# Streaming encoder step: the input projection cut into 36 units, with cache keys, gate recurrences and first queries between them

## The reference, cut to what matters

```python
# x: 64 sample rows + 16 meta rows + padding, then 1024 prompt rows (9 tiles of 128)
z = rms_norm(x, g_attn) @ w_in           # 1024 -> 1960 columns: cq, ckv, kr, gates, mq, mk, mv, mo
k, v = mla_keys_values([cache_ckv, rms_norm(z.ckv)], [cache_krope, rope(z.kr)])  # 1024 cached rows
q = rms_norm([q_nope, rope(q_rope)])     # from rms_norm(z.cq) @ w_uq
att = softmax(q k^T * scale, chunk-causal) v
b = cumsum(logf); m = running max(b, ig) # mLSTM gates, per 64-row chunk, 4 heads
h = mlstm_chunks(mq, mk, mv, ig, logf, state)
x = x + [att, rms_norm(h) * sigmoid(mo)] @ w_out
x = x + moe(rms_norm(x))                 # 32 experts, top 2
```

## Time and profile before

| | us |
|---|---|
| median of 3 runs | 1435.95 (1429.99 to 1442.3) |
| the profiled execution's own time | 1430.49 |
| its span, first to last instruction | 1428.7 |
| cache keys, to the projection's first matmul | 0 to 51.8 |
| projection | 51.8 to 294.8 |
| gates and first queries, to the first scores | 294.8 to 344.2 |
| attention and the rest | 344.2 to 1428.7 |

### The profile page before, as it was taken

One profiled execution on the slowest core, in us unless ns is written; L12 is line 12 of the kernel. 1 busy time (PEld: TensorE's weight loads), 2 busy tenths in 40 slices (PEclk: granted clock), 3 DMA queues, 4 the chain that ended last, 5 costly groups with the idle time before them and its releaser, 6 DMA issues.

```text
span 1428.7 us, 37955 instructions
## 1 busy us (share of the span) xinstructions
PE 1284.4 (90%) x16430; PEld 968.5 (68%) x16430; DVE 426.9 (30%) x873; ACT 333.7 (23%) x775; POOL 229.9 (16%) x318
## 2 busy tenths in 40 slices
PE   5899999955899999999999859999898989988995
PEld 2444444423666567666567559999898988988985
DVE  2210001036555446445444651111111111111110
ACT  4310010023544445454454200000001001000010
POOL 3100000003221222122120111111112111111101
PEclk9999999976989999999999979999999999999998
DMA  8012111050120122012030946999999999999992
GB/s 304 15 43 86 43 43 71 28 209 26 51 75 16 60 76 76 16 61 70 4 123 21 416 148 238 362 371 373 362 376 375 386 378 381 381 378 376 381 391 76
DMA packets 39709, 273.74 MB, mean 192 GB/s; under 512 B 9208, under 2 KB 13176, under 8 KB 27340
## 3 DMA queue, kind: packets, MB, share of 16 engines
q1 hardware_dynamic: 32944, 253.78, 45.9%
q0 software_dynamic: 6400, 17.84, 5.2%
q10 hardware_dynamic: 288, 1.05, 0.2%
HBM read 246.32 MB, written 30.48 MB: 194 GB/s over the span
## 4 chain that ended last, share of the span: by engine, by line
PE 69%; DMA 14%; issue 7%; DVE 4%; ACT 3%; POOL 2%; SPq 1%; POOLq 0%; ACTq 0%; DVEq 0%
PE psum L795 17%; PE psum L1058 16%; DMA arena<-in_w 12%; PE psum L1084 9%; PE psum L910 7%; PE psum L949 4%; PE psum L981 3%; PE psum L961 2%; PE psum L749 2%; PE psum L855 2%; PE psum L1094 1%; PE psum L764 1%; PE psum L1049 1%; POOL small L1461 1%; PE psum L896 1%
## 5 line engine op out<-in xcount | busy, mean ns | idle before, releaser
L1058 PE MATMUL psum<-arena 128*64 128x80 f32 (+1 forms) x8192 | 330.3, 243 | 31.3 <-DMA arena<-in_w 28.0
L1058 PEld LDWEIGHTS psum<-arena 128*64 128x64 f32 x8192 | 319.6, 142 | 41.6 <-issue 37.3
L795 PE MATMUL psum<-arena 128*128 128x512 f32 (+1 forms) x576 | 238.1, 574 | 0.6 <-DVE arena L1672 0.6
L795 PEld LDWEIGHTS psum<-arena 128*128 128x128 f32 x576 | 108.8, 190 | 124.2 <-issue 124.2
L1084 PE MATMUL psum<-arena 128*64 128x80 f32 (+1 forms) x4096 | 158.8, 239 | 5.3 <-issue 5.3
L1084 PEld LDWEIGHTS psum<-arena 128*64 128x64 f32 x4096 | 155.0, 139 | 6.1 <-issue 6.1
L910 PE MATMUL psum<-arena 128*128 128x512 f32 x288 | 127.0, 594 | 1.7 <-DVE arena L1912 1.0
L1418 ACT ACTIVATE arena<-psum,slot_gate 96x1024 f32<-96x1024 f32 x32 | 35.5, 1111 | 354.6 <-PE psum L1094 354.6
L749 PE MATMUL psum<-ident,arena 128*128 128x128 f32 (+1 forms) x432 | 65.2, 286 | 46.9 <-DVE arena L1766 18.2
L910 PEld LDWEIGHTS psum<-arena 128*128 128x128 f32 x288 | 53.3, 190 | 63.0 <-issue 61.4
L749 PEld LDWEIGHTS psum<-ident,arena 128*128 128x128 f32 (+1 forms) x432 | 50.8, 139 | 64.4 <-DVE arena L1653 19.8
(11 more groups left out here) (233 smaller groups left out, 1280.2 us busy)
## 6 DMA issues: line engine op xcount, KB each, us to landing
arena<-in_w SPq DMA_DIRECT2D x96, 2048.0 KB, 17.3
arena<-in_x_rows SPq DMA_DIRECT2D x18, 512.0 KB, 5.5
z_rows<-arena SPq DMA_DIRECT2D x9, 980.0 KB, 4.5
arena<-in_w_in SPq DMA_DIRECT2D x1, 7840.0 KB, 23.4
arena<-z_rows SPq DMA_DIRECT2D x9, 768.0 KB, 5.8
arena<-in_w_out SPq DMA_DIRECT2D x1, 4096.0 KB, 17.1
out_y<-arena SPq DMA_DIRECT2D x8, 512.0 KB, 2.6
xn_rows<-arena SPq DMA_DIRECT2D x8, 512.0 KB, 3.0
```

What stands on the lines that cost most here:

```text
L795: ins = pe.matmul(o[:, 0:hi - lo], xT[s][:, k, :], w_in[:, k, lo:hi], start=(k == 0), stop=(k == KD - 1))
L1058: ins = pe.matmul(o[c:c + CT, j * EB:j * EB + rows], w[:, k, j * P + c:j * P + c + CT], x[:, k, 0:rows], start=(k == 0), stop=(k == KD - 1))
```

## The change

The loop of the projection is replaced by 37 steps, i from -1 to 35. Step i has unit i (a tile of rows times one column chunk) and the small work `early(i)`. Units 0 to 8 are chunk 0 of the nine tiles, units 9 to 35 the other chunks, tile by tile. Steps -1 to 7 hold the cache keys, 1 to 9 the gate transposes of each tile, 11 to 18 the gate arithmetic, 19 to 28 the first tile's queries and keys and the decays (`cd`). Rows arrive transposed from DRAM (`xT_rows`) beside the plain rows, so `x_transposes` is gone; DVE scales them in SBUF (`xT_scale`). `w_in` comes chunk by chunk. Plain rows are still loaded for their squares, now by ACT's own DMA queue. Even units are emptied by ACT, odd ones by DVE, through four banks, and stored one by one. `w_out`, `g_mh` and `w_route` are loaded only after the last unit; the waits for them go to n = 1.

```diff
+UNITS = [(n, 0) for n in range(NT)] + [(n, c) for n in range(NT) for c in (1, 2, 3)]
+UBANK = (0, 1, 2, 4)
...
+def early(i):
+    if i < 0:
+        return cache_step(0) + cache_step(1)
+    m = NC
+    return (cache_step(i + 2) if i < NC else []) + [("ga", i - 1)] * (1 <= i <= NT) + {
+        19: [("cd", 0), ("cqT", 0), ("cn", 0)], 20: [("ckvT", m)], 21: [("q0", 0), ("q1", 0)],
+        22: [("kn", m), ("v", m), ("qsum", 0), ("ksum", m)], 25: [("kq", m)], 26: [("qTa", 0), ("qTb", 0)],
+        27: [("kTa", m), ("kTb", m), ("cqT", 1)], 28: [("cn", 1)],
+    }.get(i, [])
...
         @block.sync
+            load_xT(0)
+            load_w(0)
+            load_xT(1)
+            for dst, src in ((g_cq, "g_cq"), (g_ffn, "g_ffn"), (g_qk[:, 0:1], "g_q"), (g_qk[:, 1:2], "g_k"), (b_gate, "b_gate"),
+                             (mstate, "state_m")):
+                sp_.dma_start(dst, T[src]).then_inc(gains_in, 16)
+            sp_.dma_start(b_route, T["b_route"].to_broadcast([P, NG + NE])).then_inc(gains_in, 16)
+            sp_.dma_start(gate_rows, T["gate_rows"]).then_inc(gate_in, 16)
+            load_xT(2)
+            load_xT(3)
...
+            for n in range(4, 7):
+                load_xT(n)
+            load_w(1)
...
+            load_w(2)
+            load_w(3)
...
+            for i, (n, c) in enumerate(UNITS):
+                lo, hi = Z_CHUNKS[c]
+                wait_unit_read(sp_, i)
+                sp_.dma_start(z_dram[n * P:(n + 1) * P, lo:hi], zst[i % 4][:, 0:hi - lo]).then_inc(z_out[i % 4], 16)
+                if i == 17:
+                    sp_.wait_ge(z_full, 18)
+                    sp_.wait_ge(x_ssq, NT)
+                    sp_.wait_ge(kk_ok, NC)
+                    unit_stored(0)
+                    load_latents(0)
+                    sp_.dma_start(w_uq, T["w_uq"].rearrange("(k p) n -> p k n", p=P)).then_inc(wuq_in, 16)
...
+            sp_.wait_ge(z_full, len(UNITS))
+            sp_.dma_start(g_mh, T["g_mh"].to_broadcast([P, HM * DV])).then_inc(gmh_in, 16)
             sp_.dma_start(w_out, T["w_out"].rearrange("(k p) n -> p k n", p=P)).then_inc(wout_in, 16)
...
         @block.tensor
+            def z_unit(i):
+                n, c = UNITS[i]
+                w, at_ = chunk_width(c), KD * Z_CHUNKS[c][0]
+                pe.wait_ge(xT_ok, n + 1)
+                pe.wait_ge(win_in[c], 16)
+                if i >= 4:
+                    wait_unit_read(pe, i - 4)
+                o = unit_bank(i)
+                for k in range(KD):
+                    ins = pe.matmul(o[:, 0:w], xT[n][:, k, :], w_in[:, at_ + k * w:at_ + (k + 1) * w],
+                                    start=(k == 0), stop=(k == KD - 1))
+                ins.then_inc(z_full, 1)
...
+            for i in range(-1, len(UNITS)):
+                if i >= 0:
+                    z_unit(i)
+                for key in early(i):
+                    step(key)
...
         @block.scalar
+            load_x(0)
+            load_x(1)
+            for i in range(-1, len(UNITS)):
+                if i >= 0 and i % 2 == 0:
+                    z_take(i)
+                for key in early(i):
+                    fill_work(key)
+                if i < 0:
+                    x_squares(0)
+                if 1 <= i + 2 < NT:
+                    if i + 3 < NT:
+                        load_x(i + 3)
+                    x_squares(i + 2)
+                if i == 11:
+                    gate_logs()
+                if i == 18:
+                    gate_exps()
...
         @block.gpsimd
+            for i in range(-1, len(UNITS)):
+                if i < 0:
+                    kv_rstd_of(0)
+                    row_rstd(0)
+                if i + 2 <= NC:
+                    row_rstd(i + 2)
+                if 0 <= i and i + 1 < NC:
+                    kv_rstd_of(i + 1)
+                for key in early(i):
+                    pool_work(key)
...
         @block.vector
+            def xT_scale(n):
+                dve.wait_ge(xT_in[n], 16)
+                TT(xT[n], xT[n], bc(g_attn, [P, KD, P]), ALU.mult).then_inc(xT_ok, 1)
...
+            for i in range(-1, len(UNITS)):
+                if 0 <= i < NC:
+                    kv_norm(i)
+                if i >= 0 and i % 2:
+                    z_take(i)
+                if i < 0:
+                    for n in range(3):
+                        xT_scale(n)
+                elif i + 3 < NT:
+                    xT_scale(i + 3)
+                if i + 1 < NC:
+                    kv_sums(i + 1)
+                if i == 12:
+                    scale_gains()
+                if i == 13:
+                    gates_log()
+                if i == 14:
+                    gates_max()
+                if i == 16:
+                    gates_rows()
+                if i == 17:
+                    gates_end()
...
+                    if (n, h) == (1, 0):
+                        dve.wait_ge(wout_in, 32)
                         link(TT(w_route, w_route, bc(g_ffn, [P, KD, NG + NE]), ALU.mult))
```

More of the change, by code:

```diff
@@ L177, in pe_fills @@
     order = []
-    for c in range(NC + 2):
-        order += cache_step(c)
-    for n in range(-1, NT + 1):
+    for i in range(-1, len(UNITS)):
+        order += [key for key in early(i) if key[0] not in NO_BANK]
+    for n in range(NT + 1):
         if n >= 1:
@@ L193, in pe_fills @@
     return fills, used
+def early(i):
[7 more added lines that the diff above has]
+    }.get(i, [])
 def filler(n, h):
-    now, nxt, old = 0 <= n < NT, n + 1 < NT, n >= 1
+    now, nxt, old = n < NT, n + 1 < NT, n >= 1
     m = NC + n + 1
[L207 to L212, removed]
     return {
@@ L321, in build @@
         A = Area(7 * PART)
-        w_out = A(KD, D)
+        mlstm_at = A.at
+        qb, kb = A(HM, P), A(HM, P)
+        kw = kb
+        vaug = A(HM, CAUG)
+        chunk_mask = A(P)
+        state_at = A.at
+        state = [A(HM, CAUG) for _ in range(2)]
         w_route = A(KD, NG + NE)
-        after_weights = A.at
         mixT = A(KD, P)
@@ L343, in build @@
         g_mh = A(HM * DV)
[L344 to L349, removed]
+        w_out_at = ARENA - KD * D
+        assert A.at <= w_out_at, A.at
+        w_out = Area(w_out_at)(KD, D)
         A = Area(mixing)
@@ L531, in ahead, with unit_bank, chunk_width, wait_unit_read @@
             return value if isinstance(value, int) else eng.snap(value)
[L533 to L545, removed]
+        def unit_bank(i):
+            return bank(UBANK[i % 4])
+        def chunk_width(c):
+            return Z_CHUNKS[c][1] - Z_CHUNKS[c][0]
+        def wait_unit_read(eng, i):
+            eng.wait_ge(zd_read if i % 2 else za_read, i // 2 + 1)
         def load_part(eng, dst, src, row, signal):
@@ L607, in _ @@
[L607 to L618, removed]
@@ L845, in step @@
                     key_values(n, what)
+                elif what == "ga":
+                    wait_unit_read(pe, n)
+                    o = open_bank(key)
+                    for g in range(2):
+                        ins = pe.transpose(o[0:HM, g * P:(g + 1) * P], gat[:, n, g * HM:(g + 1) * HM], ident[:])
+                    filled(ins, key)
+                elif what == "cd":
+                    pe.wait_ge(g_ok, 1)
+                    pe.wait_ge(mixw_in, 16 * 4)
+                    o = open_bank(key)
+                    for h in range(HM):
+                        ins = pe.matmul(o[:, h * NCH:(h + 1) * NCH], pick[:, h, :], dec4, start=True, stop=True)
+                    filled(ins, key)
                 elif what == "cqT":
@@ new lines, in z_take @@
+            def z_take(i):
+                n, c = UNITS[i]
+                act.wait_ge(z_full, i + 1)
+                act.wait_ge(x_rstd, n + 1)
+                if i >= 4:
+                    act.wait_ge(z_out[i % 4], 16 * (i // 4))
+                o, w = unit_bank(i), chunk_width(c)
+                if c == 0:
+                    act.activation(gat[:, n], o[:, Z_GATE:Z_GATE + 2 * HM], ACT.Copy, scale=xrs[:, n:n + 1])
+                act.activation(zst[i % 4][:, 0:w], o[:, 0:w], ACT.Copy, scale=xrs[:, n:n + 1]).then_inc(za_read, 1)
@@ L2202 @@
         "g_attn": a["g_attn"].reshape(KD, P).T,
-        "w_in": _np.concatenate(cols, axis=1),
+        "xT_rows": x.reshape(NT, P, KD, P).transpose(0, 3, 2, 1).reshape(NT * P, D),
+        "w_in": _np.concatenate([by_chunk(lo, hi) for lo, hi in Z_CHUNKS], axis=1),
         "g_cq": a["g_cq"].reshape(QL // P, P).T,
```

422 lines of the change are left out of this document (172 added, 250 removed).

## The result

| | before | changed |
|---|---|---|
| median, us (range, runs) | 1432.97 (1427.87 to 1442.3, 4) | 1375.19 (1373.17 to 1375.97, 4) |
| ratio of times, 95% interval | | 0.9588 [0.9533, 0.9642] |
| span of the profiled execution | 1428.7 | 1373.5 |
| first scores | 344.21 | 291.59 |
| from there to the end | 1084.5 | 1081.9 |

Of the later kernels, two of `e10`'s four runs (1482.45 and 1484.4) and one of `e11`'s, the profiled one (1430.17), were over 1.5% above their kernel's fastest and count as slow: medians, ranges and ratios go without them.

A forecast was written before the change was run, and what follows sets the result against it. PE bounds the projection; neighbouring stages leave it idle. Scores at 26.0 + 261.1 + 0.8 + 2 + 2 = 291.9, 52.3 earlier, plus 3.7 at full clock: span 1428.7 - 56.0 = 1372.7, median 1380 us, range 1367 to 1403.

The forecast's parts named there:

- S: Start of projection unit 1, from which PE's list sets the pace: 26.0 us, bounds 23 and 37.
- Rival (a): Late start: small loads hold SP and rows meet the backlog; unit 1 at 37 us, time 1394; chance 0.20.
- PE's work, 261.1: PE's list after unit 1 starts: units, cache steps, gate transposes, first queries and keys, 261.1 us in all.
- 4.8 for eviction, backlog and group changes: Added between PE's list and first scores: 0.8 us emptying unit 35, 2 for rows' backlog, 2 for group changes.
- Scores at 291.9: First attention scores after the projection begin at 291.9 us in place of 344.2, 52.3 earlier.
- Does the small work hide?: Under the projection units, the closest loop takes 6.9 us against PE's 8.0, hiding with 1.1 us to spare.
- `w_out` at 313, needed at 327: Load after the last unit lands about 313 us, asked for at 327: cost 0 with 14 us to spare.
- 1081 to the end: From first scores to the end: 1081 us in place of 1084.5, work there otherwise moved rigidly.
- Rival (b), POOL held by DVE: In the cache-key loop, DVE's SBUF scales push POOL, costing 0 to 7 us, time 1387; chance 0.10.
- (c): A wait keeps gates and first queries behind the units; 33 us idle stays, time 1413; chance 0.06.
- (d): Late plain rows stop PE in each of seven steps, with cold unit starts: time 1490; chance 0.03.
- (e): No change: late start and loads at 18 us, time within 14 us of 1436; chance 0.03.

The follow-up runs named there:

- e10: Changed kernel plus 36 transposes of 32x32 on PE while it waits for its first loads; 1448.02 and 1449.17 us, slow runs left out.
- e11: Changed kernel with PE's row transposes put back and 72 32x32 transposes in front; median 1401.52 us, its slow profiled run of 1430.17 left out.
- e1: Changed kernel with the eight small loads on SP moved behind `xT_rows` 2 and 3; median 1364.95 us.
- e2: Changed kernel with only the load `gate_rows` moved behind `xT_rows` 3 on SP; 1372.68 us, one run.
- e3: Changed kernel with DVE doing the first sums before scaling the second and third tiles, loads unchanged; median 1365.0 us.
- e7: Changed kernel with ACT asking for plain rows in the step that uses them, not a step ahead; median 1391.61 us.
- e8: Changed kernel with PE's row transposes put back ahead of chunk 0's units, beside rows that come transposed anyway; median 1413.96 us.
- e9: Changed kernel plus 72 transposes of 32x32 on PE while it waits for its first loads; median 1405.36 us.

## Why the prediction was right, and where it wasn't

1. *What bounds the kernel.* Right. PE without a hole from 35 to 290 us at granted clock 1.00; both stages that left it idle are gone.
2. *Unit 0 near 15.* 15.51, forecast 15.3.
3. *S, the start of unit 1, 26.0.* Missed: 31.27, inside its bounds of 23 to 37. The step that was mis-sized is the landing of `xT_rows` 2: by 5.68 MB over 402 GB/s I had 18.1, it was 23.3. Both the rate and the bytes were off. The small loads ahead of it cost two microseconds of nearly empty DMA engines (`e1`, `e2`; with all of them behind, the tile was in at 17.6), and when it landed 6.8 MB had moved, since loads issued behind it ran beside it. The 7.9 us from there to unit 1 were right: 7.9 (23.35 to 31.27). Rival (a) named the culprit, by the wrong way (SP held for 2.3 us a load, where it was 0.25 to 0.50), and gave twice the price: 11 us on S against 5.3.
4. *Cold start.* Not in the forecast: unit 1 took 7.16 in place of 5.70, 1.5 us.
5. *PE's work, 261.1, and 4.8 for eviction, backlog and group changes.* From 31.27 to 291.59 are 260.3, of which 1.5 is the cold start: 258.9 in place of 265.9, 7.0 less. The 2 for the rows' backlog was 0: to landing they took a median of 4.2 us, and no one waited. The 2 for group changes was 0: the chain shows them back to back. The 0.8 was 0.9. Some 3 more are in the sum of the work: a cache step costs 0.11 + 1.72 + 0.87 = 2.70 in the chain, not the 3.07 that I read from two timeline rows, 2.2 over six steps.
6. *Scores at 291.9.* 291.59, but by two errors that cancel: 5.3 late and 1.5 cold against 7.0 that wasn't spent. That the total came out is luck. A forecast of S without the error would have ended 7 us too late, and `e3`, with unit 1 at 23.88, shows it: scores at 282.90.
7. *Does the small work hide?* Right. DVE's and ACT's gate arithmetic never made PE wait. The tightest place is step 7, where `kTa` starts within 0.1 us of its keys; it is by `e7` that one sees how near the loop is.
8. *`w_out` at 313, needed at 327.* Landed at 307, no wait.
9. *1081 to the end.* 1081.9, and the first groups of scores and queries 2.08 and 2.78. So the span is 1373.5 against 1372.7. Nearly all of the 4.8 us between the forecast of 1380 and the median of 1375.2 is the last term of the sum, 5.5 from the profiled execution to the median, taken over from the kernel before. Here it was nothing (1375.4 and 1375.2), and the runs spread over 2.8 us, not 12.
10. *Rival (b), POOL held by DVE.* It is there and doesn't count. While DVE scaled from 28.67 to 29.88, POOL's `L1493` took 1.02 us and ended with it; further on it takes 0.19. That is the rule of the Trainium skill (SBUF — State Buffer, "Who interferes with whom"), and the trace agrees. In the steps behind, DVE scales while POOL is idle, as forecast.
11. *Rivals (c), (d), (e).* None came. (d)'s mechanism works if provoked (`e7`); one step of lead prevents it.

The step on which I laid least weight, that the part behind the scores moves rigidly, held here, but not by anything in the argument: `e8`, `e9` and `e10`, with the same code there, had it 29 to 74 us longer, and so had `e11` in its longest run, by 48.5.

## What to carry to other kernels

When small chains are laid under a stage that one engine fills, the forecast is that engine's list plus its starting point. Here the list was 7 us too long and the start 5.3 too early; what could be won back lay in the start: look there for an instruction in some engine's order that waits for a later load than its successors need. When comparing kernels with loops beside a saturated stream, compare the instruction packets and the "issue" waits first: a difference behind the edit of tens of microseconds may come from where the loop lies and not from what was edited. And two repairs of one wait don't add.

## What the hardware showed that was not expected

- Eight small loads ahead of a 512 KB one left the DMA engines at 38 GB/s for 2 us, and the large one landed at 23.3 us; with the small ones behind it, at 17.6 (`e1`).
- 36 tiny transposes, costing nothing where they ran, made the kernel 73 us slower (1448.0 and 1449.2 against 1375.2), with 120 instruction packets in place of 56 and all of the loss in loops hundreds of microseconds later (`e10`). PE stops there for 4 to 7 us at a time, at the same matmul of the loop, while its packets arrive.
- A DMA issue on SP, mostly 0.4 us, can hold it far longer when much stands ahead: `g_attn` 3.76 us at 3.66, the first latent store behind `w_out` 10.22 us at 294.06. No engine waited for the second. The first lies on the chain that ended last, though the DMA engines were moving 359 to 414 GB/s meanwhile. What the length goes by isn't shown.
